# Sums of w_down's weight blocks made in DRAM by GpSimd's copying and adding DMAs

## The reference, cut to what matters

```
h = rmsnorm(x, ffn_norm[l])
gate = jnp.einsum('bsd,df->bsf', h, w_gate[l])      # 512x2048 by 2048x5632
up = jnp.einsum('bsd,df->bsf', h, w_up[l])
x = x + jnp.einsum('bsf,fd->bsd', jax.nn.silu(gate) * up, w_down[l])   # 512x5632 by 5632x2048
return rmsnorm(x, final_norm)
```

## Time and profile before

| | |
|---|---|
| median of three runs | 1999.18 us |
| profiled execution, its own time | 1998.61 us |
| span of that execution | 1996.8 us |
| granted TensorE clock | 0.999 |
| TensorE (PE) busy | 1985.3 us, 99% |
| VectorE (DVE) busy | 1613.5 us, 81% |
| ScalarE (ACT) busy | 1092.1 us, 55% |
| GpSimd (POOL) busy | 146.1 us, 7% |
| DMA | 273.88 MB, mean 137 GB/s |

### The profile page before, as it was taken

One profiled execution on the slowest core, in us unless ns is written; L12 is line 12 of the kernel. 1 busy time (PEld: TensorE's weight loads), 2 busy tenths in 40 slices (PEclk: granted clock), 3 DMA queues, 4 the chain that ended last, 5 costly groups with the idle time before them and its releaser, 6 DMA issues.

```text
span 1996.8 us, 30319 instructions
## 1 busy us (share of the span) xinstructions
PE 1985.3 (99%) x10380; PEld 1702.8 (85%) x10380; DVE 1613.5 (81%) x2319; ACT 1092.1 (55%) x2000; POOL 146.1 (7%) x241
## 2 busy tenths in 40 slices
PE   9999999999999999999999999999999999999998
PEld 8888888888888998888888888888888888888886
DVE  5666667666766899999999999999998688697876
ACT  6455556555435655555555555555456355566643
POOL 1122222222100000000000000000000000000000
PEclk9999999999999999999999999999999999999999
DMA  8222222225234444434444434443446846546343
GB/s 300 85 75 74 74 74 75 74 69 160 76 96 136 139 138 137 136 128 138 137 137 135 135 132 136 137 135 129 137 137 220 309 135 211 181 149 226 122 131 132
DMA packets 131899, 273.88 MB, mean 137 GB/s; under 512 B 13568, under 2 KB 13600, under 8 KB 130768
## 3 DMA queue, kind: packets, MB, share of 16 engines
q1 hardware_dynamic: 119344, 233.36, 36.8%
q0 software_dynamic: 6640, 23.82, 3.0%
q10 hardware_dynamic: 5808, 15.23, 2.1%
HBM read 240.89 MB, written 31.46 MB: 136 GB/s over the span
## 4 chain that ended last, share of the span: by engine, by line
PE 97%; issue 1%; ACT 1%; DVE 1%; DMA 0%; ACTq 0%; SPq 0%; POOLq 0%; POOL 0%
PE bank L677 27%; PE bank L680 14%; PE bank L565 8%; PE bank L567 7%; PE bank L566 7%; PE bank L609 7%; PE bank L611 7%; PE bank L610 7%; PE bank L734 3%; PE bank L736 3%; PE bank L735 3%; PE bank L761 1%; PE bank L778 1%; PE bank L746 1%; PE bank L745 1%; PE bank L777 1%
## 5 line engine op out<-in xcount | busy, mean ns | idle before, releaser
L677 PE MATMUL bank<-s_two,t_hi 128*128 128x512 f32 x2352 | 557.3, 390 | 0.0
L677 PEld LDWEIGHTS bank<-s_two,t_hi 128*128 128x128 f32 x2352 | 433.5, 188 | 84.7
L1190 ACT ACTIVATE t_hi<-t_raw 128x1792 fp32r<-128x1792 f32 x176 | 302.0, 1718 | 357.7 <-DVE t_raw L1766 268.6
L1489 DVE TENSOR_TENSOR w_lo<-raw,w_hi 128x512 fp32r<-128x512 f32 x300 | 208.5, 697 | 210.7 <-ACT w_hi L963 208.9
L1772 DVE TENSOR_TENSOR t_lo<-t_raw,t_hi 128x1792 fp32r<-128x1792 f32 x176 | 355.4, 2019 | 23.5 <-ACT t_hi L1190 23.3
L963 ACT ACTIVATE w_hi<-raw 128x512 fp32r<-128x512 f32 x300 | 188.1, 629 | 264.1 <-PE bank L611 144.1
L680 PEld LDWEIGHTS bank<-s_two,t_lo 128*128 128x128 f32 x2352 | 298.8, 191 | 9.9
L680 PE MATMUL bank<-s_two,t_lo 128*128 128x256 f32 x2352 | 302.0, 283 | 0.0
L1763 DVE TENSOR_TENSOR t_raw<-t_raw 128x1024 f32<-128x1024 f32 x176 | 214.8, 1221 | 13.0 <-DMA t_raw<-in_w_gu 11.5
L565 PE MATMUL bank<-h_hi,w_hi 128*128 128x512 f32 x544 | 218.5, 402 | 0.5 <-DVE h_lo L1493 0.4
L567 PE MATMUL bank<-h_lo,w_hi 128*128 128x512 f32 x544 | 213.2, 392 | 0.0
(11 more groups left out here) (215 smaller groups left out, 3119.9 us busy)
## 6 DMA issues: line engine op xcount, KB each, us to landing
t_raw<-in_w_gu SPq DMA_DIRECT2D x348, 256.0 KB, 2.7
raw<-in_w_in SPq DMA_DIRECT2D x136, 256.0 KB, 2.6
raw<-in_w_down SPq DMA_DIRECT2D x112, 256.0 KB, 3.6
gu_mid<-part POOLq DMA_DIRECT2D x43, 512.0 KB, 2.9
gu_next<-gu_mid SPq DMA_DIRECT2D x36, 512.0 KB, 6.9
raw<-in_w_out SPq DMA_DIRECT2D x64, 256.0 KB, 3.1
fast_y<-in_w_down SPq DMA_DIRECT2D x24, 512.0 KB, 5.0
fast_z<-in_w_down SPq DMA_DIRECT2D x16, 512.0 KB, 4.4
```

The source lines that it names most:

```text
L677: mm = nc.tensor.matmul(b[:, :], t_hi[r][:, ti, q, :], both, start=d == 0 and q == 0, stop=d == DOUBLES - 1 and q == 1 and i < 4, skip_gro ...
L1190: nc.scalar.activation(t_hi[r][:, :, :, :].rearrange("p a q c -> p (a q c)"), t_raw[r][:, 1:8, :, :].rearrange("p a q c -> p (a q c)"), AC ...
L1489: nc.vector.tensor_tensor(w_lo[:, s, :], raw[:, s, :], w_hi[:, s, :].bitcast(F32), ALU.subtract).then_inc(w_lo_done, 1)
```

## The change

The sums of the weight quarters are no longer made by VectorE. A DRAM tensor `t_down` (four chunks x four sums x 1 MB) is filled from GpSimd's queue during gate/up: after the stores of tiles 8 to 13 come the six steps for chunk 1, after tiles 16 to 21 those for chunk 2, after 24 to 29 chunk 3, after 32 to 37 chunk 4. A chunk has four copies (DRAM to DRAM, 1 MB each) and four adding DMAs (`accum_op=ALU.add`, 1 MB each); steps 0 and 1 have two DMAs each, steps 2 to 5 one each. Before steps 1 to 5 GpSimd waits until the DMAs of the steps before are done, since each reads what they wrote. As the sums can only be additions, some signs move: `a_sums` and `join` add or subtract in another order, with the same number and shapes of instructions.

In w_down the six buffers x, y and z become one ring of six (`FAST_RAWS`), and each of the 14 fast units of a chunk is one load of 512 KB from `t_down` or from w_down, issued six units ahead. `f_sum` is gone; `f_high` waits for the load alone.

```diff
+FAST_RAWS = 6
+SUMMED = {P5: 0, P6: 1, P7: 2, P4: 3}
+QUARTER = {P3: (2, 2), P1: (1, 0), P2: (2, 0)}
...
+        def load_fast(c, j):
+
+            p, u, q = j // 2, j % 2, fast_count(c, j) - 1
+            if q >= FAST_RAWS:
+                sp.wait_ge(f_lo_done, q + 1 - FAST_RAWS)
+            if p in SUMMED:
+                sp.wait_ge(t_down_done, 16 * 8 * c)
+                src = t_down[c - 1, SUMMED[p], 256 * u:256 * (u + 1), :]
+            else:
+                rows, n = QUARTER[p]
+                row = 1024 * c + 512 * (rows - 1) + 256 * u
+                src = w_down2[row:row + 256, 512 * n:512 * (n + 1)]
+            sp.dma_start(fast_raw[q % FAST_RAWS][:, :, :], src.rearrange("(k p) c -> p k c", p=P)).then_inc(fast_loaded[q % FAST_RAWS], 16)
...
-            if s in (24, 25):
-                load_quarter("x", raw_x, 1, s - 24, 1, 2)
-                load_quarter("y", raw_y, 1, s - 24, 1, 0)
-            if s in (26, 27):
-                load_quarter("z", raw_z, 1, s - 26, 2, 2)
+            if 22 <= s < 22 + FAST_RAWS:
+                load_fast(1, s - 22)
...
+                if kind == "S":
+                    c2, j2 = after(c, s, FAST_RAWS)
+                    if c2 < CHUNKS:
+                        load_fast(c2, j2)
...
-                        f_sum(c2, j2)
                         a_sums(c2, j2)
...
+        def copy_t(c, p, src):
+
+            nc.gpsimd.dma_start(t_down[c - 1, SUMMED[p], :, :], src).then_inc(t_down_done, 16)
+
+        def add_t(c, p, src):
+
+            nc.gpsimd.dma_start(t_down[c - 1, SUMMED[p], :, :], src, accum_op=ALU.add).then_inc(t_down_done, 16)
+
+        def weight_sums(c, step):
+
+            done = 16 * 8 * (c - 1)
+            if step == 0:
+                copy_t(c, P5, quarter(c, 1, 0))
+                copy_t(c, P7, quarter(c, 1, 2))
+            if step == 1:
+                pool.wait_ge(t_down_done, done + 16 * 2)
+                add_t(c, P5, quarter(c, 1, 2))
+                add_t(c, P7, quarter(c, 2, 2))
+            if step == 2:
+                pool.wait_ge(t_down_done, done + 16 * 4)
+                copy_t(c, P6, t_down[c - 1, SUMMED[P5], :, :])
+            if step == 3:
+                pool.wait_ge(t_down_done, done + 16 * 5)
+                add_t(c, P6, quarter(c, 2, 2))
+            if step == 4:
+                pool.wait_ge(t_down_done, done + 16 * 6)
+                copy_t(c, P4, t_down[c - 1, SUMMED[P6], :, :])
+            if step == 5:
+                pool.wait_ge(t_down_done, done + 16 * 7)
+                add_t(c, P4, quarter(c, 2, 0))
+
         for g in range(TILES):
             store_gu(g)
             if g == 1:
                 invert(3, slice(0, NT))
+            c, step = 1 + (g - 8) // 8, (g - 8) % 8
+            if 1 <= c < CHUNKS:
+                weight_sums(c, step)
```

More of the change, by code:

```diff
@@ L115, with build @@
 HEAD = [("A", 0, 0), ("A", 1, 3), ("B", 0, 6), ("B", 1, 8)]
-def build(nc, x, x_turned, gain_cols, w_in, sinks, w_out, w_gu, w_down, final_norm, c_dist, c_lnm, c_band, c_slope, c_ident, x_mid, gu_mid, out):
+def build(nc, x, x_turned, gain_cols, w_in, sinks, w_out, w_gu, w_down, final_norm, c_dist, c_lnm, c_band, c_slope, c_ident, x_mid, gu_mid, t_down, out):
     spot = [(nc.sbuf_base + 63) // 64 * 64]
@@ L237, in build @@
     gu_next = sb("gu_next", [P, CHUNK, 2, SEQ], at=place_att)
-    fast_raw = {b: [sb(f"fast_{b}{u}", [P, 2, SEQ], at=place_att + 32768 + 4096 * (2 * i + u)) for u in range(2)]
-                for i, b in enumerate("xyz")}
+    fast_raw = [sb(f"fast_raw{r}", [P, 2, SEQ], at=place_att + 32768 + 4096 * r) for r in range(FAST_RAWS)]
     f_hi = [sb(f"f_hi{r}", [P, 2, SEQ], F32R, at=place_att + 57344 + 8192 * r) for r in range(2)]
@@ L288, in build @@
     scaled, stored = sem("scaled"), sem("stored")
-    raw_x, raw_y, raw_z = ([sem(f"fast_{b}_loaded{u}") for u in range(2)] for b in "xyz")
-    f_sum_done, f_hi_done, f_lo_done, f_used = sem("f_sum_done"), sem("f_hi_done"), sem("f_lo_done"), sem("f_used")
+    fast_loaded = [sem(f"fast_loaded{r}") for r in range(FAST_RAWS)]
+    t_down_done = sem("t_down_done")
+    f_hi_done, f_lo_done, f_used = sem("f_hi_done"), sem("f_lo_done"), sem("f_used")
     a_sum_done, a_hi_done, a_lo_done = sem("a_sum_done"), sem("a_hi_done"), sem("a_lo_done")
@@ L1351, in f_high @@
         def f_high(c, j):
-            p, u = j // 2, j % 2
             count = fast_count(c, j)
[L1355 to L1362, removed]
+            act.wait_ge(fast_loaded[(count - 1) % FAST_RAWS], 16 * ((count - 1) // FAST_RAWS + 1))
             if count > 2:
@@ L1365, in f_high @@
             nc.scalar.activation(f_hi[(count - 1) % 2][:, :, :].rearrange("p k c -> p (k c)"),
-                                 fast_raw[FAST_FROM[p]][u][:, :, :].rearrange("p k c -> p (k c)"), ACT.Copy).then_inc(f_hi_done, 1)
+                                 fast_raw[(count - 1) % FAST_RAWS][:, :, :].rearrange("p k c -> p (k c)"), ACT.Copy).then_inc(f_hi_done, 1)
         def a_high(c, j):
@@ L1911, in ahead_down @@
             split(unit // 4, unit % 4)
[L1913 to L1930, removed]
         def a_sums(c, j):
@@ L1939, in a_sums @@
                 dve.wait_ge(act_done, 8 * c + 2 * u + 6)
-                nc.vector.tensor_tensor(a_sum(j), a21, a22, ALU.add).then_inc(a_sum_done, 1)
+                nc.vector.tensor_tensor(a_sum(j), a22, a21, ALU.subtract).then_inc(a_sum_done, 1)
             elif p == P6:
                 dve.wait_ge(a_sum_done, sums_count(c, 2 * P5 + u))
-                nc.vector.tensor_tensor(a_sum(j), a_sum(j), a11, ALU.subtract).then_inc(a_sum_done, 1)
+                nc.vector.tensor_tensor(a_sum(j), a_sum(j), a11, ALU.add).then_inc(a_sum_done, 1)
             elif p == P7:
@@ L1947, in a_sums @@
                 dve.wait_ge(a_sum_done, sums_count(c, 2 * P6 + u))
-                nc.vector.tensor_tensor(a_sum(j), a12, a_sum(j), ALU.subtract).then_inc(a_sum_done, 1)
+                nc.vector.tensor_tensor(a_sum(j), a_sum(j), a12, ALU.subtract).then_inc(a_sum_done, 1)
         def f_low(c, j):
-            p, u = j // 2, j % 2
-            r = (fast_count(c, j) - 1) % 2
-            low_half(f_lo[r][:, :, :].rearrange("p k c -> p (k c)"), fast_raw[FAST_FROM[p]][u][:, :, :].rearrange("p k c -> p (k c)"),
+            q = fast_count(c, j) - 1
+            r = q % 2
+            low_half(f_lo[r][:, :, :].rearrange("p k c -> p (k c)"), fast_raw[q % FAST_RAWS][:, :, :].rearrange("p k c -> p (k c)"),
                      f_hi[r][:, :, :].rearrange("p k c -> p (k c)"), f_hi_done, fast_count(c, j), f_lo_done)
@@ L1960, in a_low, with join @@
             low_half(a_lo[r][:, :, :], a_sum(j), a_hi[r][:, :, :], a_hi_done, sums_count(c, j), a_lo_done)
-        def join(p, q, op, kept_of):
+        def join(to, p, q, op, kept_of):
             dve.wait_ge(kept, FAST_U * (CHUNKS - 2) + 2 * kept_of + 2)
-            nc.vector.tensor_tensor(m_sum[:, p, :, :], m_sum[:, p, :, :], m_sum[:, q, :, :], op).then_inc(joined, 1)
+            nc.vector.tensor_tensor(m_sum[:, to, :, :], m_sum[:, p, :, :], m_sum[:, q, :, :], op).then_inc(joined, 1)
         def add_fast(p, half, n):
@@ L2002, in down_first @@
                 if s in (26, 27):
-                    f_sum(1, s - 26)
                     a_sums(1, s - 26)
@@ L2010, in down_first @@
                 if s == 30:
-                    f_sum(1, 2)
                     a_sums(1, 2)
@@ L2050, in down @@
                 if e == 20:
-                    join(P6, P1, ALU.add, P1)
-                    join(P3, P5, ALU.add, P3)
+                    join(P6, P6, P1, ALU.subtract, P1)
+                    join(P3, P3, P5, ALU.add, P3)
                 if e == 21:
                     dve.wait_ge(joined, 2)
-                    join(P7, P6, ALU.add, P7)
-                    join(P3, P6, ALU.add, P6)
+                    join(P7, P6, P7, ALU.subtract, P7)
+                    join(P3, P6, P3, ALU.subtract, P6)
                 if e == 22:
                     dve.wait_ge(joined, 4)
-                    join(P5, P7, ALU.add, P5)
+                    join(P5, P7, P5, ALU.subtract, P5)
                     add_fast(P3, 0, 2)
@@ L2062, in down @@
                     dve.wait_ge(joined, 7)
-                    join(P7, P4, ALU.subtract, P4)
+                    join(P7, P4, P7, ALU.subtract, P4)
                     add_fast(P5, 1, 2)
@@ L2068, in down @@
                 if e == 28:
-                    join(P1, P2, ALU.add, P2)
+                    join(P1, P1, P2, ALU.add, P2)
                 if e == 29:
@@ L2196, in store_gu, with quarter @@
             nc.gpsimd.dma_start(gu_mid[g, :, :], z[:, 0:4, :].rearrange("p a c -> p (a c)")).then_inc(gu_stored, 16)
+        def quarter(c, rows, n):
+            return w_down2[1024 * c + 512 * (rows - 1):1024 * c + 512 * rows, 512 * n:512 * (n + 1)]
+        def copy_t(c, p, src):
[23 more added lines that the diff above has]
+                add_t(c, P4, quarter(c, 2, 0))
         for g in range(TILES):
```

31 lines of the change are left out of this document (1 added, 30 removed).

## The result

The changed kernel takes 2104.13 us (median of 4 runs, 2098.68 to 2104.85), the kernel before 1999.35 (4 runs): ratio 1.0519, 95% interval 1.0506 to 1.0531 (the two medians alone give 1.0524, inside it). Forecast were 2017.6 us and a range to 2060. The direction and the place were right, the size was out by a factor of almost six (+104.8 us measured, +18.4 forecast).

A forecast was written before the change was run, and what follows sets the result against it. PE was taken to bound the kernel, busy 1985.3 of 1996.8 us. Lateness of 10.8 us a chunk, less 4.8 and 1.4, gave 4.6; four chunks made +18.4 us, so 2017.6 us, with a range of 1998.5 to 2060.

The forecast's parts named there:

- 0 for `f_sum` and for the loads: w_down: 38.8 us less of DVE worth 0, as PE doesn't wait there; 8 more loads 0, between 0 and +2 us.
- The place: Gate/up: new transfers meet the pair of loads with 0.4 us of margin in 24 tiles; one lateness a tile counts.
- C: w_down: faster, from 38.8 us less of DVE; 1998.4 us, within the bound of no change; chance 0.02.
- B: Gate/up: clogged, adding DMAs fill the engines from tile to tile or past GpSimd's next wait; 2096 us; chance 0.09.
- the full tiles: Gate/up, clogged case: all eight tiles of a chunk have the full lateness, 24 us a chunk, +97 us.
- the late store: Gate/up, clogged case: two adds over about 19.5 + 7 us delay the next tile's store, and ScalarE waits for it.
- the sign that steps 1, 3 and 5 would lengthen most: Gate/up: sign of a right forecast, that the tile of 19.47 us lengthens most in the steps with adding DMAs.
- the sum's other two terms: Gate/up, per chunk: 4.8 us absorbed by DVE's idle time (0.8 a tile) and 1.4 us by PE's lead.
- the term "How late?": Gate/up: lateness of the pair, 1.2 us in three copying tiles and 2.4 in three adding ones, 10.8 a chunk.
- +1.6 and +2.8: Gate/up: landing delays of earlier loads beside 1 MB transfers, taken for copies and adds, less 0.4 us of margin.
- The ceiling: Gate/up: worst earlier load +4.4 us, so 4.0 late in all six tiles of a chunk, +71 us in all.
- The sum that I had made from both rules: Gate/up: by two Trainium skill rules, copies 1.4 us late and adds 3.2, +30 us over four chunks.

## Why the prediction was wrong

**Right, as far as the runs show it.** w_down: 0 for `f_sum` and for the loads (1999.05 us without the 32 DMAs). The place: the pair of loads behind the fourth double's `t_lo`, one lateness a tile (where a second wait shows, it is 0.8 us); C absent, and of B both the full tiles and the late store. Not quite right was the sign that steps 1, 3 and 5 would lengthen most: step 0, two plain copies, costs as much as step 3 and more than step 5. The working from lateness to time: with the lateness of the trace, 123.2 us more in 32 tiles or 30.8 a chunk, the sum's other two terms would give (30.8 - 4.8 - 1.4) x 4 = 98 us, against 105.8. Of the 4.8 a chunk, 14.7 / 4 = 3.7 us was there.

**Wrong: the term "How late?"**, 10.8 us a chunk, where DVE's waits for loads grew by 30.8. It took 1.2 us for a copying step and 2.4 for an adding one. DVE's waits in the first chunk by step were 6.7, 8.3, 3.0, 6.7, 2.5 and 5.7 us, 32.9 in all; the rows of steps 0, 1 and 2:

```profile
DVE t_raw L1739 <- DMA t_raw<-in_w_gu: 6.7, 1, 6.7
DVE t_raw L1739 <- DMA t_raw<-in_w_gu: 8.3, 2, 7.5
DVE t_raw L1739 <- DMA t_raw<-in_w_gu: 3.0, 1, 3.0
```

Three things went wrong in it:

- It added the delays that other loads had shown, +1.6 and +2.8, as if a delay were a property of the neighbour. The earlier trace rows said otherwise and I had quoted it: 511 packets of one transfer went through before the pair's own. That pair was only 1.6 us late, as I read it, because the transfer in front of it was fast (1 MB in 3.0 us) and already under way. The question was how much is in flight ahead of the load when it is issued, here a megabyte or two of slower packets. In the two runs in pieces the amount in flight was changed, with the spread over the tile that comes with it, and that is worth 88 us.
- It gave steps with two DMAs the price of one. Two copies in step 0 made 6.7 us of waiting, one copy inside `t_down` 3.0.
- The ceiling, 4.4 - 0.4 = 4.0 us, was the worst load of the trace of before, and no bound for a transfer that this trace didn't have. The longest wait was 8.2, beside the two plain copies of chunk 2. Six steps at 4.0 gave +71; the range ended even below.

The adds' own slowness, which the prediction had feared most, is 33 us of 105. In the first chunk two adds landed after 15.3 us, two copies after 9.9. On the rule of the Trainium skill's "Collectives: The Full Stack" ("The bandwidth ceiling: the fold count and why AG ≠ RS ≠ AR") that two source reads halve the rate: a packet of an add took 0.173 us for 2 KB, which is 1.9 times a load's 0.091, so the trace agrees for the packets, as far as an add in DRAM may be set beside a load. On the rule of the Trainium skill's "DMA: Bandwidth & Descriptors" ("Queues, rings and completion order") that an engine takes the queue rows in turn: the trace agrees from 1075.5 us on (373 and 353 packets), and not for the 4.5 us before (307 and 11). By that section an engine changes over only after a whole packet, which can hold several descriptors; no run here shows how the profile's packets stand to these, so how far the first stretch contradicts the rule is open. The sum that I had made from both rules, +30 us, misses for that first part.

Rival B came near with its number (2096) for a reason that doesn't hold: in the changed kernel the free tiles aren't long but short (18.9 us), and ScalarE never waits for `gu_mid`. A number that fits is no proof of its mechanism: 2096 against 2104 is luck.

**Open:** what sets the 19 packets on each engine that go ahead of a load (the queue's own depth or the order in which descriptors are handed over); why the adds' packets take 0.236 us in that stretch and 0.173 after it, and whether some of the waiting is for DRAM and not for the 16 engines, which no run tells apart; whether the 29.4 us of extra busy time of PE, at the lower clock, would cost something by themselves in a kernel whose DVE were faster.

## What to carry to other kernels

- Before traffic is added beside a stage, list that stage's loads by margin, from the end of the instruction that lets the load go to the start of the one that needs it, less the landing time. Two loads in eight with 0.4 us of margin made 105 us of loss; the same bytes were free beside the loads of the attention stage, where a block landed after up to 9.9 us and no engine waited for it.
- Price the lateness by what is in flight ahead of the load when it is issued, not by a landing time seen beside some other transfer. Pieces with a wait between them bound it (2020 against 2108 us), as long as nothing that matters queues behind those waits (2100).
- Work taken from an engine on which PE doesn't wait was worth nothing here: 38.8 us of `f_sum`.

## What the runs showed of the hardware that I had not expected

- A load of the hardware queue, issued 2.7 us after an adding DMA of GpSimd's queue, had almost no packet through for 4.5 us (11 against 307), and only then about one in two (353 against 373).
- Adding in DRAM: 0.173 us for a packet of 2 KB, two adds of 1 MB landing after 14.1 to 15.3 us beside gate/up's loads; a copy from `t_down` to `t_down`, both sides contiguous, landed after 6.3 to 6.7 us.
- The granted clock of PE was 0.94 over a tile in which PE had stood for two waits of 1.6 and 4.4 us; between 902 and 905 us, right after the second, it was 0.50, and 14 matmuls took 3.36 us that had taken 1.83.
